# A two-layer encoder trunk on one core: the front end's weights in 20 buffers, 16 of them in the still empty gather ring, and 16 projections of the second block moved ahead of the first expert step

## The chip, the cores and the metric

The kernel runs on one core of a Trainium2 chip, in float32. The time is the device time of one execution in microseconds (us). Before the change it is 1650.69 us, the median of 3 runs (1648.89 to 1652.69).

The engines are TensorE (PE; PEld is its loading of weights), VectorE (DVE), ScalarE (ACT), GpSimd (POOL) and SyncE (SP). SP and ACT start plain transfers, POOL starts the indirect ones. All transfers run on the core's 16 DMA engines.

## The reference, cut to what matters

272 tokens (16 meta tokens and 256 of the input) of width 1024 pass through two layers. Each layer is a mixer and then a PEER layer, in which every token picks, for each of 8 heads, 16 of 16384 experts and reads their two rows of 1024 numbers.

```python
h = concatenate([meta, x])                         # 272 tokens, width 1024
for i in range(2):
    y = rmsnorm(h, mix_norm_g[i])
    h = h + (mixer_ab(y, ...) if i == 0 else mixer_conformer(y, ...))
    y = rmsnorm(h, ffn_norm_g[i])
    h = h + peer(y, peer_w_q[i], peer_sub_keys[i], peer_u[i], peer_v[i])
return rmsnorm(h, final_norm_g)[:, 16:272]

def mixer_ab(y, w_in, conv_w, w_out):
    q, k, v, gate_b, gate_c, h = split(y @ w_in, 6)  # w_in: 1024 x 3072
    a = stick_breaking_attention(q, k, v)            # 8 heads of 64
    b = gate_b * causal_conv3(gate_c * h, conv_w)
    return concat(a, b) @ w_out                      # 1024 x 1024

def peer(y, w_q, sub_keys, u, v):
    q = y @ w_q                                      # 1024 x 2048
    # top 16 of 128 keys on either side, top 16 of the 256 pairs -> expert, gate
    act = gate * gelu(sum(u[expert] * y))            # a dot of 1024 per expert
    return sum(act * v[expert])
```

## The kernel before, in words

**Layout.** Activations lie transposed: 128 partitions by (8 chunks of the width, tokens). A weight matrix of 1024 rows is cut into chunks of 128 columns, 512 KB each; one chunk is one transfer, and one projection of 8 matmuls (16 in the trace, where each float32 matmul has two records). The tokens are cut into a first block (A) of 128 and a second block (B) of 144.

**Front end.** The front end of block A runs alone: 24 chunks of the input projection (`inA`) with the attention between them, 8 of the output projection (`outA`), 16 of the query projection (`qA`). Then come the router's scores for the first 16 tokens (`scores(0)`, line 821 on PE), its top-k on DVE (`route_best`, `route_pairs`, `route_experts`, lines 1129 to 1185) and with `s_idx` the first gathers on POOL (line 382).

**Steps.** 33 steps `n` follow, 16 tokens each (16 tokens by 8 heads are the 128 partitions). A step takes 16 gathers of 1 MB into the ring `ring` of R = 12 slots. DVE makes a dot per gather (line 1191), ACT the gelu per quarter of a step (line 633), DVE the coefficients (lines 1202 and 1207), and PE sums the second halves of the rows (`values`, line 842), which frees 4 slots (`s_vm`). So gather `i` waits, from the 13th on, for the `values` of gather `i - 12`. `rows` (line 830) repeats the tokens of a step over the heads for the dots; `gates` (line 451) is the softmax's exponential on ACT, for which `route_pairs` of the next step waits.

**Work of block B beside the steps.** The table `FRONT` gives block B's front end quarter by quarter: `FRONT[u]` is issued by PE in quarter `u` (`u = 4 n + q`), and by ACT and DVE in the same order. Entries -3 to -1 run ahead of step 0. `inB` 0 to 11 stood there, `inB` 12 to 15 in quarters 0 and 1. Later the second layer's mixer runs in the same way (`side`).

**Weights.** `STREAM` lists all weight chunks in the order of use. SP walks it (line 352) with NB = 4 buffers (`wring`): a chunk's transfer waits until the projection that used its buffer is done (`s_proj`). The 16 chunks of `qA` alone had a place of their own, ring slots 4 to 11, and were started as 8 transfers of 1 MB between `inA` chunks (line 356). Slots 0 to 3 of the ring are block A's working memory until the gathers begin.

**Engine order.** Each engine has one fixed order of instructions; there is no scheduler. A wait holds everything that is behind it on its engine.

The lines that set this (the transfers' wait, then the gathers' wait):

```python
            for i, (row, job) in enumerate(STREAM):
                if i >= NB:
                    sp.wait_ge(s_proj, STREAM[i - NB][1] + 1)
                sp.dma_start(wring[:, i % NB, :, :]..., wall[row]).then_inc(s_w[i % NB], 16)
...
                    if i >= R:
                        pool.wait_ge(s_vm, i - R + 1)
```

## Time and profile before

| | |
|---|---|
| median of 3 runs | 1650.69 us |
| the profiled execution's own time | 1650.49 us |
| its span in the trace | 1648.7 us |
| busy: PE, DVE, ACT, POOL | 64%, 68%, 28%, 31% of the span |
| granted TensorE clock, mean of the span | 0.788 |
| moved by DMA | 649.84 MB, mean 394 GB/s |
| gathers | 528, 553.68 MB together |
| first gather issued | 126.50 us |

The time stands 1.8 us above the span, for what lies around it. The busy shares are means over stages with different limits, so they are read by stage: the front end up to 126.5 us, then the steps. "DMA" in a row is the mean busy share of the 16 DMA engines, and it can read slightly above 1.

### The profile page before, as it was taken

To read this page: it belongs to the slowest core of one execution; us is meant where nothing else is said; L and a number is where in the kernel's file an instruction comes from. 1 tells how busy PE (TensorE), PEld (TensorE's weight loads), DVE (VectorE), ACT (ScalarE), POOL (GpSimd) and SP (SyncE) were. 2 spreads that over 40 slices of the span, in tenths; PEclk is the share of its full clock that TensorE was granted. 3 is DMA by queue.
4 is the path that set the end of the run, shared out by engine and by line. 5 is a ranking of instruction groups with operands and counts; after the bars stand their busy time and mean duration, and the time that the engine had idled before them with its cause. 6 is when DMAs were issued, how large, how long until landed. Compare 5 with 4: busy or idle time off the path is not lost.

```text
span 1648.7 us, 19969 instructions
## 1 busy us (share of the span) xinstructions
PE 1048.9 (64%) x6936; PEld 710.0 (43%) x6936; DVE 1113.8 (68%) x3119; ACT 462.7 (28%) x953; POOL 503.8 (31%) x541
## 2 busy tenths in 40 slices
PE   7896777657744477776685456785766444544444
PEld 7896553434511156655463135664554111111111
DVE  2434658867557765887745766797756777777764
ACT  4101344302111133853221122873221211111110
POOL 0002323433233322332323332333323333333330
PEclk9999877878976689887897579887888655555666
DMA  9819999999999999899999999999999999999995
GB/s 333 328 65 394 418 420 386 421 419 419 417 420 422 421 419 414 348 411 384 417 417 417 422 420 417 371 401 398 411 418 418 422 421 422 421 422 421 419 421 212
DMA packets 105892, 649.84 MB, mean 394 GB/s; under 512 B 11456, under 2 KB 15552, under 8 KB 38208
## 3 DMA queue, kind: packets, MB, share of 16 engines
q0 software_dynamic: 76032, 553.68, 81.3%
q1 hardware_dynamic: 26272, 92.81, 14.5%
q10 hardware_dynamic: 3488, 2.08, 0.4%
q8 instruction: 55, 0.90, 0.2%
q14 instruction: 45, 0.37, 0.1%
HBM read 647.48 MB, written 1.05 MB: 393 GB/s over the span
## 4 chain that ended last, share of the span: by engine, by line
DMA 43%; PE 24%; DVE 16%; issue 5%; ACT 5%; POOL 5%; DVEq 2%; another core or an unknown queue 1%; POOLq 0%; ACTq 0%
DMA ring<-in_uv_dram,expert 31%; DMA wring<-in_wall_dram 12%; PE ps L659 10%; DVE ring L1191 7%; PE ps L842 7%; POOL ring L382 5%; ACT side L560 2%; PE ps L744 2%; DVE side L1246 2%; PE ps L855 1%; PE ps L666 1%; PE ps L883 1%; PE ps L830 1%; DVE picked L1183 1%
## 5 line engine op out<-in xcount | busy, mean ns | idle before, releaser
L1191 DVE CUSTOM_DVE_ANT_0 ring<-ring,ps 128x1024 f32<-128x1024 f32 x528 | 635.2, 1218 | 338.7 <-DMA ring<-in_uv_dram,expert 246.5
L382 POOL DMA_INDIRECT ring<-in_uv_dram,expert x528 | 501.8, 950 | 1110.9 <-PE ps L842 862.8
L842 PE MATMUL ps<-ring,mix 128*32 128x512 f32 x2112 | 366.3, 829 | 306.9 <-DVE mix L1207 303.8
L659 PE MATMUL ps<-yT,wring 128*128 128x128 f32 (+1 forms) x2048 | 279.0, 297 | 95.9 <-DMA wring<-in_wall_dram 58.5
L659 PEld LDWEIGHTS ps<-yT,wring 128*128 128x128 f32 x2048 | 262.9, 203 | 121.6 <-DMA wring<-in_wall_dram 64.8
L842 PEld LDWEIGHTS ps<-ring,mix 128*32 128x32 f32 x2112 | 67.8, 135 | 504.7 <-DVE mix L1207 364.4
L633 ACT ACTIVATE gel<-dots 128x4 f32<-128x4 f32 x132 | 27.1, 205 | 745.3 <-DVE dots L1191 667.6
L855 PE MATMUL ps<-sel,osb 128*128 128x16 f32 x528 | 76.9, 289 | 74.2 <-ACT osb L619 71.1
L855 PEld LDWEIGHTS ps<-sel,osb 128*128 128x128 f32 x528 | 73.6, 223 | 114.5 <-ACT osb L619 110.4
L560 ACT ACTIVATE side<-ident,params 128x128 f32<-128x128 f32 x310 | 97.3, 389 | 17.9 <-PE ps L883 16.3
L830 PE MATMUL ps<-ident,yg 128*128 128x128 f32 x264 | 52.3, 364 | 72.4 <-DVE dots L1191 72.4
L883 PE MATMUL ps<-side 128*128 128x128 f32 x620 | 85.5, 301 | 7.3 <-ACT side L560 6.7
L883 PEld LDWEIGHTS ps<-side 128*128 128x128 f32 x620 | 81.4, 214 | 16.3 <-issue 16.3
L830 PEld LDWEIGHTS ps<-ident,yg 128*128 128x128 f32 x264 | 44.0, 193 | 74.3 <-issue 74.1
L659 PE MATMUL ps<-side,wring 128*128 128x128 f32 (+1 forms) x512 | 67.8, 294 | 9.9 <-ACT side L586 7.9
L659 PEld LDWEIGHTS ps<-side,wring 128*128 128x128 f32 x512 | 65.1, 205 | 17.5 <-ACT side L586 9.7
L633 ACT ACT_TABLE_LOAD x51 | 65.4, 1283 | 1.5
L1246 DVE SCALAR_TENSOR_TENSOR side<-side,params 128x128 f32<-128x128 f32 x180 | 54.0, 347 | 0.0
L619 ACT COPY osb<-ps 128x1024 f32<-128x1024 f32 x33 | 33.3, 1009 | 46.2 <-PE ps L842 41.4
L1202 DVE SCALAR_TENSOR_TENSOR coef<-gel,grec,gexp 128x4 f32<-128x4 f32 x132 | 28.6, 217 | 24.3 <-ACT gel L633 20.3
L1191 DVE DVE_READ_ACCUMULATOR2_ANT dots<- 128x1 f32 x528 | 43.6, 83 | 0.0
L451 ACT ACT_TABLE_LOAD x33 | 42.3, 1283 | 0.9
(201 smaller groups left out, 954.4 us busy)
## 6 DMA issues: line engine op xcount, KB each, us to landing
wring<-in_wall_dram SPq DMA_DIRECT2D x160, 512.0 KB
ring<-in_uv_dram,expert POOLq DMA_INDIRECT x528
ring<-in_wall_dram SPq DMA_DIRECT2D x8, 1024.0 KB, 9.7
out_dram<-fo ACTq DMA_DIRECT2D x16, 64.0 KB
hT<-in_xT_dram ACTq DMA_DIRECT2D x1, 576.0 KB, 12.0
hT<-in_xT_dram SPq DMA_DIRECT2D x2, 256.0 KB, 5.0
params<-in_smalls_dram ACTq DMA_DIRECT2D x1, 430.0 KB, 4.4
```

What stands on the lines that cost most here:

```text
L382: pool.indirect_dma_start(out=ring[:, i % R, :], out_offset=None, in_=uv, in_offset=bass.IndirectOffsetOnAxis(ap=expert[:, n % 2, k:k + 1] ...
L451: act.activation(gexp[:, n % 2, :], topv[:, :], ACT.Exp, bias=negm[:, :], accum_out=gsum[:, n % 2:n % 2 + 1]).then_inc(s_exp, 1)
L560: act.activation(diag[:, j % NDIAG, :], ident[:, :], ACT.Identity, scale=convT[:, c, k:k + 1]).then_inc(s_dg, 1)
L619: act.copy(osb[:, :], po.rearrange("p a b -> p (a b)")).then_inc(s_oe, 1)
L633: act.activation(gel[:, 4 * q:4 * q + 4], dots[:, 4 * q:4 * q + 4], ACT.Gelu).then_inc(s_gel, 1)
L659: last = pe.matmul(ps[:, m % 2, 0:w], wring[:, i % NB, c, :], rhs(c), start=(c == 0), stop=(c == C - 1))
L830: last = pe.transpose(yrep[:, c * P:(c + 1) * P], yg[:, c, :, :].rearrange("p h t -> p (h t)"), ident[:, :])
L842: mm = pe.matmul(po[32 * j:32 * j + 32, half, :], mix[:, k, :], ring[:, slot, D + 512 * half:D + 512 * (half + 1)], start=(q == 0), stop=( ...
L855: last = pe.matmul(pt[:, c, :], osb[:, c * P:(c + 1) * P], sel4[:, :], start=True, stop=True)
L883: mm = pe.matmul(ps[:, m % 2, 0:P], diag[:, j % NDIAG, :], gz[:, c, o0 + k:o0 + k + P], start=(k == 0), stop=(k == CK - 1))
L1191: nc.vector.tensor_tensor_reduce(out=row, in0=row, in1=yrep, scale=1.0, scalar=0.0, op0=ALU.mult, op1=ALU.add, accum_out=dots[:, k:k + 1]) ...
L1246: ins = nc.vector.scalar_tensor_tensor(out=cv[:, c, :], in0=src, scalar=tap, in1=cv[:, c, :], op0=ALU.mult, op1=ALU.add)
```

## The change

The diff has four parts.

1. The weights of the front end go through 20 buffers: the 4 of `wring` and 16 in ring slots 4 to 11, two to a slot. `qA` joins `STREAM` (the 1 MB transfers and `s_wq` are gone). `BUFFER[i]` is the buffer of entry `i`: up to `EARLY` (the entry behind `inB` 15) they go round 20 buffers, so placed that `inB` 0 to 15 fall into the ring's 16; after it they go round the 4 of `wring`.
2. `FRONT` has quarters -4 to -1 with `inB` 0 to 15, four each; quarters 0 and 1 have no projections now. On ACT `gates(0)` comes behind all 16 instead of between them.
3. Gathers 4 to 11 wait for the second of the two `inB` projections whose weights lie in their slot (`FREE = 4`).
4. ACT starts only the first 100 columns of `params` at once; block B's part of `hT` (576 KB) and the other 760 columns (conv taps and keys) are started behind the two squares, and have `s_par2`.

```diff
-    FRONT = {-3: [("inB", k) for k in range(4)], -2: [("inB", k) for k in range(4, 8)], -1: [("inB", k) for k in range(8, 12)],
-             0: [("inB", 12), ("inB", 13)], 1: [("inB", 14), ("inB", 15)],
-             2: [("inB", 16), ("inB", 17), ("vt", 0), ("vt", 1)],
+    FRONT = {u: [("inB", 16 + 4 * u + k) for k in range(4)] for u in range(-4, 0)}
+    FRONT |= {2: [("inB", 16), ("inB", 17), ("vt", 0), ("vt", 1)],
@@
-    WQ0 = 32
+    STREAM += [(32 + k, JOB["qA", k]) for k in range(16)]
@@
+    FREE = 4
+    EARLY = LOADED[JOB["inB", 15]] + 1
+    BUFFER = [(i - EARLY) % (NB + 16) if i < EARLY else (i - EARLY) % NB for i in range(len(STREAM))]
+    BEFORE = [[j for j in range(i) if BUFFER[j] == BUFFER[i]] for i in range(len(STREAM))]
@@
+        def weights_at(i):
+            b = BUFFER[i]
+            if b < NB:
+                return wring[:, b, :, :]
+            return flat[:, (4 + b) * D:(5 + b) * D].rearrange("p (c n) -> p c n", n=P)
@@ sync
-                if i >= NB:
-                    sp.wait_ge(s_proj, STREAM[i - NB][1] + 1)
-                sp.dma_start(wring[:, i % NB, :, :].rearrange("p c n -> p (c n)"), wall[row]).then_inc(s_w[i % NB], 16)
-                if 8 <= i < 24 and i % 2 == 0:
-                    j = i // 2 - 4
-                    sp.dma_start(wq0[:, 2 * j:2 * j + 2, :, :].rearrange("p k c n -> p k (c n)"),
-                                 wall[WQ0 + 2 * j:WQ0 + 2 * j + 2].rearrange("k p n -> p k n")).then_inc(s_wq[j], 16)
+                if BEFORE[i]:
+                    sp.wait_ge(s_proj, STREAM[BEFORE[i][-1]][1] + 1)
+                sp.dma_start(weights_at(i).rearrange("p c n -> p (c n)"), wall[row]).then_inc(s_w[BUFFER[i]], 16)
@@ gpsimd
+                    elif i >= FREE:
+                        pool.wait_ge(s_proj, JOB["inB", 2 * (i - FREE) + 1] + 1)
@@ scalar
-            act.dma_start(params[:, :], smalls).then_inc(s_par, 16)
-            act.dma_start(hT[:, :, TA:L], ...).then_inc(s_x[2], 16)
+            act.dma_start(params[:, 0:PAR["conv"]], smalls[:, 0:PAR["conv"]]).then_inc(s_par, 16)
             for i in range(2): ...                     # the two squares
+            act.dma_start(hT[:, :, TA:L], ...).then_inc(s_x[2], 16)
+            act.dma_start(params[:, PAR["conv"]:NPAR], smalls[:, PAR["conv"]:NPAR]).then_inc(s_par2, 16)
@@
+            act.wait_ge(s_par2, 16)
             rows(0)
-            front(-3)
-            front(-2)
+            for u in range(-4, 0):
+                front(u)
             gates(0)
-            front(-1)
@@ tensor, ahead of the steps
+            pe.wait_ge(s_par2, 16)
             scores(0)
-            front(-3)
+            front(-4)
             scores(1)
             rows(0)
-            front(-2)
-            front(-1)
+            for u in range(-3, 0):
+                front(u)
```

PE before, from the last projections of `qA` (L744) to the second `values` (L842): L821 is `scores`, L830 `rows`, L659 with `yT` 128x144 the projections of block B, 8 matmuls each.

```order
L744 MATMUL ps<-ring 128x128 x120
L821 MATMUL ps<-params,qT 128x128 x2
L659 MATMUL ps<-yT,wring 128x144 x32
L821 MATMUL ps<-params,qT 128x128 x2
L830 MATMUL ps<-ident,yg 128x128 x8
L659 MATMUL ps<-yT,wring 128x144 x80
L842 MATMUL ps<-ring,mix 32x512 x8
L659 MATMUL ps<-yT,wring 128x144 x16
L842 MATMUL ps<-ring,mix 32x512 x8
L659 MATMUL ps<-yT,wring 128x144 x16
```

The same place of the changed kernel, whose line numbers are 3 to 9 higher (L668 is the projection, L845 `values`):

```order
L668 MATMUL ps<-ring,wring 128x128 x32
L824 MATMUL ps<-params,qT 128x128 x2
L668 MATMUL ps<-yT,ring 128x144 x32
L824 MATMUL ps<-params,qT 128x128 x2
L833 MATMUL ps<-ident,yg 128x128 x8
L668 MATMUL ps<-yT,ring 128x144 x96
L845 MATMUL ps<-ring,mix 32x512 x16
L668 MATMUL ps<-yT,wring 128x144 x16
```

Between `rows(0)` and the first `values` stand 12 projections instead of 10, and between the first two `values` none instead of 2.

POOL before, with the semaphores that each row waits for, from the last memset to step 1's first gathers:

```order
L374 MEMSET mix 128x512
L382 DMA ring<-in_uv_dram,expert 128x2048 [waits s_idx]
L382 DMA ring<-in_uv_dram,expert 128x2048 x11
L382 DMA ring<-in_uv_dram,expert 128x2048 [waits s_vm] x4
L382 DMA ring<-in_uv_dram,expert 128x2048 [waits s_vm,s_idx]
```

And in the changed kernel:

```order
L380 MEMSET mix 128x512
L391 DMA ring<-in_uv_dram,expert 128x2048 [waits s_idx]
L391 DMA ring<-in_uv_dram,expert 128x2048 x3
L391 DMA ring<-in_uv_dram,expert 128x2048 [waits s_proj] x8
L391 DMA ring<-in_uv_dram,expert 128x2048 [waits s_vm] x4
L391 DMA ring<-in_uv_dram,expert 128x2048 [waits s_vm,s_idx]
```

Eight of the first 12 gathers have got a wait on the projections.

ACT before, from the copy of `rows(0)` (L447) to the first gelu (L633), with L467 the emptying of an `inB` projection and L451 `gates(0)`:

```order
L447 COPY yg<-yT 128x1024 [waits s_y]
L467 COPY side<-ps 128x144 [waits s_proj] x8
L451 ACT_TABLE_LOAD
L451 ACTIVATE gexp,gsum<-topv,negm 128x16 [waits s_top]
L467 COPY side<-ps 128x144 [waits s_proj] x4
L447 COPY yg<-yT 128x1024 [waits s_yr,s_y]
L633 ACT_TABLE_LOAD
L633 ACTIVATE gel<-dots 128x4 [waits s_dot]
```

And in the changed kernel:

```order
L456 COPY yg<-yT 128x1024 [waits s_y,s_par2]
L476 COPY side<-ps 128x144 [waits s_proj] x16
L460 ACT_TABLE_LOAD
L460 ACTIVATE gexp,gsum<-topv,negm 128x16 [waits s_top]
L456 COPY yg<-yT 128x1024 [waits s_yr,s_y]
L642 ACT_TABLE_LOAD
L642 ACTIVATE gel<-dots 128x4 [waits s_dot] x3
```

`gates(0)` now follows 16 copies instead of 8, and nothing but the copy of `rows(1)` stands between it and the first gelu.

## Rows read from the trace of the kernel before

**Rows 1.** The page: GB/s in 40 slices of 41.2 us, and the gathers' queue.

```profile
GB/s 333 328 65 394 418 420 386 421 419 419 417 420 422 421 419 414 348 411 384 417 417 417 422 420 417 371 401 398 411 418 418 422 421 422 421 422 421 419 421 212
...
q0 software_dynamic: 76032, 553.68, 81.3%
```

**Rows 2.** Windows: busy us of PE, PEld, DVE, ACT, POOL, clock, DMA share, GB/s.

```profile
0.00:126.50 126.50, 112.23 (x942) 108.35 (x943) 45.31 (x151) 25.85 (x39) 1.77 (x12) 0.99 0.67 242
126.50:1648.70 1522.20, 936.70 (x5996) 601.68 (x5995) 1068.45 (x2969) 436.86 (x914) 502.07 (x529) 0.77 0.99 407
126.50:162.60 36.10, 23.68 (x164) 21.98 (x167) 14.88 (x47) 6.79 (x16) 11.44 (x12) 0.91 0.99 404
100.00:118.00 18.00, 17.52 (x156) 17.36 (x155) 3.68 (x16) 0.00 (x0) 0.00 (x0) 1.00 0.00 1
30.00:32.00 2.00, 2.00 (x13) 1.77 (x13) 0.29 (x1) 0.00 (x0) 0.00 (x0) 0.50 1.03 422
250.00:280.00 30.00, 19.04 (x116) 9.70 (x112) 27.57 (x76) 16.65 (x22) 11.81 (x12) 0.73 0.96 374
```

**Rows 3.** Waits up to 125 us; DVE in 193 to 248 (us, times, longest).

```profile
PEld ps L659 <- DMA wring<-in_wall_dram: 8.7, 7, 2.1
...
DVE ring L1191 <- DMA ring<-in_uv_dram,expert: 11.0, 8, 2.5
```

**Rows 4.** Timeline of PE: start, us, what, records, idle before.

```profile
9.69 10.88 PE L659 MATMUL ps<-yT,wring 128*128 128x128 f32 x96
...
28.69 2.67 PE L659 MATMUL ps<-yT,wring 128*128 128x128 f32 x16 [1.92 <-DMA wring<-in_wall_dram]
...
32.45 6.04 PE L659 MATMUL ps<-yT,wring 128*128 128x128 f32 x48
...
67.70 2.13 PE L719 MATMUL ps<-side,ones 128*128 128x144 f32 x16
...
116.16 0.68 PE L821 MATMUL ps<-params,qT 128*128 128x128 f32 x4 [0.47 <-DVE qT L1046]
...
161.78 1.92 PE L842 MATMUL ps<-ring,mix 128*32 128x512 f32 x16
...
259.90 3.64 PE L842 MATMUL ps<-ring,mix 128*32 128x512 f32 x16 [5.37 <-DVE mix L1207]
```

**Rows 5.** Timeline of DVE: start, then steps 0 to 2.

```profile
5.66 1.77 DVE L947 TENSOR_SCALAR yT<-hT,params 128x128 f32<-128x128 f32 x8 [5.66 <-DMA hT<-in_xT_dram]
...
126.04 0.17 DVE L1185 TENSOR_TENSOR expert<-picked 128x16 uint32<-128x16 f32 x1
...
148.89 0.14 DVE L1199 RECIPROCAL grec<-gsum 128x1 f32<-128x1 f32 x1
157.15 0.22 DVE L1202 SCALAR_TENSOR_TENSOR coef<-gel,grec,gexp 128x4 f32<-128x4 f32 x1 [8.11 <-ACT gel L633]
...
168.74 0.22 DVE L1202 SCALAR_TENSOR_TENSOR coef<-gel,grec,gexp 128x4 f32<-128x4 f32 x1
...
193.23 1.22 DVE L1191 CUSTOM_DVE_ANT_0 ring<-ring,ps 128x1024 f32<-128x1024 f32 x1 [1.46 <-PE ps L830]
...
247.83 1.22 DVE L1191 CUSTOM_DVE_ANT_0 ring<-ring,ps 128x1024 f32<-128x1024 f32 x1 [7.77 <-PE ps L830]
```

**Rows 6.** Timeline of POOL: gathers 0 and 12, and one of step 2.

```profile
126.50 1.09 POOL L382 DMA_INDIRECT ring<-in_uv_dram,expert  x1 [123.92 <-DVE expert L1185]
...
163.96 0.94 POOL L382 DMA_INDIRECT ring<-in_uv_dram,expert  x1 [22.66 <-PE ps L842]
...
263.80 0.94 POOL L382 DMA_INDIRECT ring<-in_uv_dram,expert  x1 [7.22 <-PE ps L842]
```

**Rows 7.** Timeline of ACT: an inB evacuation, and gates(0).

```profile
120.80 0.28 ACT L467 COPY side<-ps 128x144 f32<-128x144 f32 x1 [1.68 <-PE ps L659]
...
144.07 1.28 ACT L451 ACT_TABLE_LOAD   x1
```

**Rows 8.** The page's transfers: KB each, median us to landing.

```profile
hT<-in_xT_dram ACTq DMA_DIRECT2D x1, 576.0 KB, 12.0
```

More of the change, by code:

```diff
@@ L78, in hybrid_trunk @@
              9: [("av", 1), ("z", 6), ("z", 7), ("suf", 4), ("suf", 5)],
-             11: [("av", 2), ("suf", 6), ("suf", 7)], 13: [("av", 3)], 19: [("ssB", 0)]}
+              11: [("av", 2), ("suf", 6), ("suf", 7)], 13: [("av", 3)], 19: [("ssB", 0)]}
     for k in range(8):
@@ L113, in hybrid_trunk @@
                 STREAM.append((row + k, JOB[name % w, k]))
+    FREE = 4
+    EARLY = LOADED[JOB["inB", 15]] + 1
+    BUFFER = [(i - EARLY) % (NB + 16) if i < EARLY else (i - EARLY) % NB for i in range(len(STREAM))]
+    BEFORE = [[j for j in range(i) if BUFFER[j] == BUFFER[i]] for i in range(len(STREAM))]
+    assert all(BUFFER[LOADED[JOB["inB", k]]] == NB + k for k in range(16))
     ctx = ExitStack()
@@ L231, in hybrid_trunk @@
         ct = carve(AC, TA)
-        wq0 = flat[:, 8 * D:24 * D].rearrange("p (k c n) -> p k c n", c=C, n=P)
+        def weights_at(i):
[3 more added lines that the diff above has]
+            return flat[:, (4 + b) * D:(5 + b) * D].rearrange("p (c n) -> p c n", n=P)
         ps = ctx.enter_context(nc.psum_tensor("ps", [P, 8, 512], f32))
@@ L251, in hybrid_trunk @@
         s_par = sem("s_par")
-        s_w = [sem(f"s_w{b}") for b in range(NB)]
-        s_wq = [sem(f"s_wq{i}") for i in range(8)]
+        s_w = [sem(f"s_w{b}") for b in range(NB + 16)]
+        s_par2 = sem("s_par2")
         s_const = sem("s_const")
@@ L391, in _ @@
         def _(act):
-            act.dma_start(params[:, :], smalls).then_inc(s_par, 16)
-            act.dma_start(hT[:, :, TA:L], xT[:, C * TA:C * L].rearrange("p (c t) -> p c t", t=TB)).then_inc(s_x[2], 16)
+            act.dma_start(params[:, 0:PAR["conv"]], smalls[:, 0:PAR["conv"]]).then_inc(s_par, 16)
             for i in range(2):
@@ L400, in _ @@
                 act.activation(sq[:, cs, :], hT[:, cs, 0:TA], ACT.Square).then_inc(s_sq, 1)
+            act.dma_start(hT[:, :, TA:L], xT[:, C * TA:C * L].rearrange("p (c t) -> p c t", t=TB)).then_inc(s_x[2], 16)
+            act.dma_start(params[:, PAR["conv"]:NPAR], smalls[:, PAR["conv"]:NPAR]).then_inc(s_par2, 16)
             act.wait_ge(s_const, 6)
@@ L654, in chunk @@
                 i = LOADED[m]
-                pe.wait_ge(s_w[i % NB], 16 * (i // NB + 1))
+                pe.wait_ge(s_w[BUFFER[i]], 16 * (len(BEFORE[i]) + 1))
                 if m >= 2:
@@ L658, in chunk @@
                 for c in range(C):
-                    last = pe.matmul(ps[:, m % 2, 0:w], wring[:, i % NB, c, :], rhs(c), start=(c == 0), stop=(c == C - 1))
+                    last = pe.matmul(ps[:, m % 2, 0:w], weights_at(i)[:, c, :], rhs(c), start=(c == 0), stop=(c == C - 1))
                 last.then_inc(s_proj, 1)
@@ L736, in _ @@
             for k in range(16):
-                m = JOB["qA", k]
-                if k % 2 == 0:
-                    pe.wait_ge(s_wq[k // 2], 16)
                 if k == 0:
                     pe.wait_ge(s_hg2, C)
-                pe.wait_ge(s_bank[m % 2], m // 2)
-                for c in range(C):
-                    last = pe.matmul(ps[:, m % 2, 0:TA], wq0[:, k, c, :], hg2[:, c, :], start=(c == 0), stop=(c == C - 1))
-                last.then_inc(s_proj, 1)
+                chunk("qA", k, lambda c: hg2[:, c, :], TA)
                 if k == 0:
@@ L1021, in _ @@
                     log_weights(1)
+            dve.wait_ge(s_par2, 16)
             for c in range(C):
```

## The prediction, as it was put on record before the changed kernel ran

> **What bounds the kernel now.** I read the page first. Its row of GB/s [rows 1] shows 417 to 422 in most slices, with one hole, 65 in the third (82 to 124 us), and weaker slices later (386, 348, 371). I take 419 as the full rate. So I split the span where the first gather is issued, at 126.50 us [rows 6]: 242 GB/s before it and 407 behind it [rows 2]. Before it PE is busy 112.2 of 126.5 us, and from 100 to 118 us it is busy 17.5 of 18.0 us while DMA moves nothing. After it PE, DVE and ACT all have idle time and DMA has none to speak of (0.99). Two rules follow. In the front end TensorE sets the time. In the steps the bytes do: 528 gathers of 553.68/528 = 1.0486 MB [rows 1], 2.50 us each at the full rate, and each weight chunk of 0.524 MB, 1.25 us. A chunk that is moved out of the steps into the idle time before the first gather is worth 1.25 us, and a front end that ends earlier is worth what it ends earlier, as long as DMA doesn't run dry after it.
>
> **1. The front end, up to `scores(0)`, at 116.16 us before [rows 4].**
> - Start: PE begins behind the first half of `hT`, which DVE awaits until 5.66 us [rows 5]. It shares the engines with the 440 KB of `params`. Of these 51 KB are left, and 0.39 MB at the 350 to 400 GB/s of a loaded start is 1.0 us. Since they interleave I take 0.7 us off; bounds 0 and 1.3.
> - Weights: the loads of TensorE wait 8.7 us for `wring` in 7 waits, 2.1 the longest [rows 3]. They come about because four buffers are too few beside the eight 1 MB transfers that take half of the rate. With 20 buffers in the order of use, chunk k has landed at about 5 + 1.3 k us and is wanted at 9 + 1.8 k (96 records, 6 chunks, in 10.88 us [rows 4]). All 8.7 us go.
> - Clock: behind the wait of 1.92 us the granted clock is 0.50 in 30 to 32 us [rows 2]. That is 1.2 GHz, the lower level. There 16 records took 2.67 instead of 1.81 us and 48 took 6.04 instead of 5.44 [rows 4], 1.5 us together. Without the wait I take it off too.
> - What is late next: DVE. Between `inA` 13 and 19 four convolution chains and two weight steps lie on it, by the timeline nearly as long as PE's seven projections. I add 0.6 us; bounds 0 and 1.5. The stage has room for these terms: `inA` takes 67.70 - 9.69 = 58.0 us [rows 4], 24 chunks of 1.81 us are 43.4, and of the other 14.6 the waits and the clock are 10.2; the rest is the attention's own matmuls.
> - `outA` and `qA` run at PE's pace and keep it; taking `qA`'s weights from one buffer or another costs the same.
>
> Sum: -0.7 - 8.7 - 1.5 + 0.6 = -10.3 us (bounds -7 and -11.5). `scores(0)` stands at 105.9, the first index 10.0 us behind it as before (126.04 [rows 5]), the first gather at 116.2.
>
> **2. The 16 projections.** They take 1.96 us each (1.68 + 0.28 [rows 7]). Four run from 106.4 to 114.3, then `scores(1)` and `rows(0)`, 1.4 us, then twelve to 139.3. Before, PE made 10 of them by 161.8, waiting for weights that came between gathers.
> - Gather g (4 to 11) waits for `inB` 2(g-4)+1. Those end at 110.4, 114.3, 119.6, then every 3.9 us up to 139.3. The gathers are served every 2.50 us from about 118.3 (issue 1.1 us [rows 6], then about 1 us to the bytes, my estimate), so gather 11 has its turn only at 145.9. Each wait ends before its turn and costs nothing. Queued behind them on POOL are only later gathers.
> - `gates(0)` now stands behind all 16 on ACT, and DVE's `route_pairs(1)` waits for it. From its table load to DVE's reciprocal took 144.07 to 149.03 [rows 5, 7], 5.0 us. So 139.6 + 5.0 = 144.6, coefficients until 145.1 (12.4 us earlier than 157.15 [rows 5]), `values` at 145.2.
> - `values` to the gather that it frees took 2.2 us (161.78 to 163.96) with a fast clock and 3.9 us (259.90 to 263.80) behind 5.37 us of idle PE [rows 4, 6]. PE is idle for 5.9 us here, so 3.9: gather 12 is issued at 149.1, its bytes flow at 150.9, but the first twelve end at 148.4. **DMA is dry for about 2.5 us.** That is new.
> - Gathers 12 to 15 end at 160.9. Gather 16 needs the second `values`: 11.6 us behind the first on DVE (157.15 to 168.74 [rows 5], no gather awaited there), 156.9, + 3.9 = 160.8, bytes at 162.6. Dry again, 1.7 us. From there the weights of `inB` 20 on join and the freeing runs ahead. Bounds for both together: 0 and 9 us.
>
> **3. The bytes.** Before, 242 x 126.5 = 30.6 MB had moved at the first gather. The changed kernel has moved 68 chunks (48, 16, and `inB` 16 to 19 in `wring`) and 1.6 MB of inputs, 37.2 MB, at 116.2. I compare at 162.6: before 30.6 + 404 x 36.1 us = 45.2 MB [rows 2], changed 37.2 + 16 x 1.0486 = 54.0 MB. It is ahead by 8.8 MB, 21.0 us at 419 GB/s.
>
> **4. Does the lead survive?** Only if the chain over DVE, ACT and PE is as far ahead. Its first coefficients are 12.4 us earlier. Step 1's first dot came 24.5 us behind 168.74, with gather waits in it; kept whole it falls at 156.3 + 24.5 = 180.8, before at 193.23. Step 1 lasted 54.6 us to 247.83 [rows 5], of which DVE waited 11.0 us for gathers [rows 3]. Those have landed now, so step 2 starts at 224.4, 23.4 us earlier. The chain leads by more than DMA. Before, it was late there: 374 GB/s in 250 to 280 us [rows 2], (419 - 374) x 30 / 419 = 3.2 us lost. I take 2.5 us of them back (bounds 0 and 3.2). From step 3 on both kernels are the same, shifted; the weak slices later are made by chains that shift with it.
>
> Total: 1650.5 (the profiled execution's own time; the median is 0.2 us more) - 21.0 - 2.5 = **1627 us**. Ends: no dry time and all dips back, -5; front end at -7, no dips back, dry time doubled, +10. So 1621 to 1637.
>
> **The rivals.**
> - *The chain was the bound, not the bytes.* DMA's 0.99 then only shows queues kept full, and steps 0 and 1 keep their length: the gain is step 1's first dot, 12.4 us, 1638. For it: DVE waits 7.8 us for `rows` at 247.83 [rows 5] and DMA sags there. Against: DVE waited 11.0 us for gathers in the same step.
> - *The front end keeps its length.* The deep weight queue on SP starves block B's `hT`, which ACT now starts 5 us later, and ACT stands before the scores' copies: -10.3 shrinks to about -1, and as fewer gathers have been overtaken, 1636. For it: alone among the 4 first transfers it took 12.0 us to land [rows 8], and up to 16 chunks are ahead of it now. Against: in those 12 us it and `params` got 1.0 MB of some 4 (333 GB/s [rows 1]) beside a queue that was never empty; at that share it lands at about 15 us and is wanted at 20. The Trainium skill, "DMA: Bandwidth & Descriptors", section "Queues, rings and completion order", says that each DMA engine takes turns between the queues that have work, packet by packet, so a deep queue would not starve ACT's; the trace agrees as far as that share goes.
> - *Slower: the clock falls in the long dense run.* PE has 130 us without a gap, and if the clock is halved from `scores(0)` on, a projection takes 3.9 us. Each of the 16 that runs so delays the first `values` by 1.96 us, and DMA is dry for all of it, since only 12 gathers lie before it and the last of them wait too. All 16: 31 us, 1658. It is slower than before from the twelfth on. For it: 0.50 at 30 to 32 us, 0.73 in the steps [rows 2]. Against: the clock is 0.99 over the front end with PE 89% busy, and 1.00 in 100 to 118; each low value follows an idle PE. The Trainium skill, "TensorE: Matmul & The Clock Gate", section "Part 1: The HAM clock gate", puts it the same way round: the gate throttles an idle array and work opens it. By that page there is no such loss on one core, and by these rows neither.
> - *More than forecast:* no dry time and the later weak slices (348, 371) shrink as well: 12 us stand in these two, a third of them back and -5 give 1618.
>
> **How the numbers follow.** Forecast 0.60; the chain 0.12; the front end 0.10; more than forecast 0.11; the halved clock 0.04; something I have not thought of, near no change, 0.03. What the measurement can tell from no change is 0.2%, 3.3 us. Faster 0.93, same 0.02, slower 0.05. The range 1617 to 1638 takes in the forecast's 1621 to 1637, the front-end rival and half each of the chain's and of the larger gain.
>
> **What would show it.** In the profile of the changed kernel: no wait of PE for `wring` before 67 us and `scores(0)` at 104.7 to 109; the first gather 10.3 us behind it; DMA at full rate until about 148 us, then one or two gaps below 3 us each; the slice of 247 to 288 us at 410 or more; the same 407 to 410 GB/s behind the first gather, over a shorter stretch. I am wrong if waits for `s_proj` hold POOL while DMA is dry, if `gates(0)` delays the first `values` past 150 us, or if the span from the first gather to the end, 1522 us before, is not about 13 us shorter.

## The result

The changed kernel takes 1626.5 us (median of 4 runs, 1625.2 to 1627.5) where the kernel before takes 1649.8 (the 3 runs given above and one more, 1645.7 to 1652.7): ratio 0.986, 95% interval 0.984 to 0.988. The profiled execution took 1626.37 us, with a span of 1624.6. The forecast was 1627.

### The profile page after: what moved, and what is told of

Same layout as the page of the kernel before. It is cut to its first block, busy times and chain, and to the rows that moved or that the text cites. A ratio compares the mean times of both kernels' runs of the same rounds, so it can differ in the third digit from the quotient of the medians.

```text
span 1624.6 us, 19989 instructions
## 1 busy us (share of the span) xinstructions
PE 1046.7 (64%) x6936; PEld 712.2 (44%) x6936; DVE 1113.1 (69%) x3119; ACT 462.3 (28%) x953; POOL 502.6 (31%) x541
## 3 DMA queue, kind: packets, MB, share of 16 engines
q1 hardware_dynamic: 26400, 92.81, 14.7%
## 4 chain that ended last, share of the span: by engine, by line
DMA 40%; PE 26%; DVE 16%; POOL 5%; ACT 5%; issue 5%; DVEq 2%; POOLq 0%; ACTq 0%
DMA ring<-in_uv_dram,expert 33%; PE ps L668 13%; DMA wring<-in_wall_dram 8%; DVE ring L1197 7%; PE ps L845 7%; POOL ring L391 5%; ACT side L569 2%; PE ps L858 2%; DVE side L1252 2%; PE ps L675 1%; ACT L460 1%; PE ps L833 1%; DVE picked L1189 1%; DVE mix L1213 1%; PE ps L886 1%
## 5 line engine op out<-in xcount | busy, mean ns | idle before, releaser
L845 PE MATMUL ps<-ring,mix 128*32 128x512 f32 x2112 | 365.6, 827 | 311.4 <-DVE mix L1213 311.2
L845 PEld LDWEIGHTS ps<-ring,mix 128*32 128x32 f32 x2112 | 67.4, 134 | 509.7 <-DVE mix L1213 367.8
L668 PE MATMUL ps<-yT,wring 128*128 128x128 f32 (+1 forms) x1472 | 205.6, 301 | 71.8 <-DMA wring<-in_wall_dram 43.7
L668 PEld LDWEIGHTS ps<-yT,wring 128*128 128x128 f32 x1472 | 193.6, 207 | 94.6 <-DMA wring<-in_wall_dram 48.1
L858 PE MATMUL ps<-sel,osb 128*128 128x16 f32 x528 | 84.0, 304 | 78.6 <-ACT osb L628 78.6
L858 PEld LDWEIGHTS ps<-sel,osb 128*128 128x128 f32 x528 | 80.6, 241 | 116.7 <-ACT osb L628 116.7
L668 PE MATMUL ps<-yT,ring 128*128 128x128 f32 (+1 forms) x576 | 69.3, 282 | 0.0
L668 PEld LDWEIGHTS ps<-yT,ring 128*128 128x128 f32 x576 | 68.6, 193 | 1.2 <-issue 1.1
L668 PE MATMUL ps<-side,wring 128*128 128x128 f32 (+1 forms) x448 | 59.7, 296 | 10.7 <-ACT side L595 8.1
L668 PEld LDWEIGHTS ps<-side,wring 128*128 128x128 f32 x448 | 57.3, 206 | 17.9 <-ACT side L595 10.0
## 6 DMA issues: line engine op xcount, KB each, us to landing
ring<-in_wall_dram SPq DMA_DIRECT2D x52, 512.0 KB, 13.2
hT<-in_xT_dram ACTq DMA_DIRECT2D x1, 576.0 KB, 15.9
params<-in_smalls_dram ACTq DMA_DIRECT2D x1, 380.0 KB, 19.2
```

Of the source, the lines that this page charges most:

```text
L668: last = pe.matmul(ps[:, m % 2, 0:w], weights_at(i)[:, c, :], rhs(c), start=(c == 0), stop=(c == C - 1))
L845: mm = pe.matmul(po[32 * j:32 * j + 32, half, :], mix[:, k, :], ring[:, slot, D + 512 * half:D + 512 * (half + 1)], start=(q == 0), stop=( ...
L858: last = pe.matmul(pt[:, c, :], osb[:, c * P:(c + 1) * P], sel4[:, :], start=True, stop=True)
```

## The profile after

The page: GB/s in 40 slices (of 40.6 us), the gathers' queue, and two of the transfers of ACT's queue.

```profile
GB/s 371 355 230 380 417 411 408 419 421 417 418 422 421 421 418 417 352 421 407 420 416 421 421 419 417 353 409 394 415 418 405 422 422 422 421 422 422 421 421 194
...
q0 software_dynamic: 76032, 553.68, 82.4%
...
hT<-in_xT_dram ACTq DMA_DIRECT2D x1, 576.0 KB, 15.9
...
params<-in_smalls_dram ACTq DMA_DIRECT2D x1, 380.0 KB, 19.2
```

Against [rows 1] the third slice holds 230 GB/s instead of 65: that is the hole before the first gather, and most of what changed. The first two slices rose too (371 and 355 for 333 and 328), and the seventh (408 for 386); the fourth fell a little (380 for 394), and it holds the new dry time. The weak slices later (352 and 353 for 348 and 371) stand where they stood.

Windows (busy us of PE, PEld, DVE, ACT, POOL, clock, DMA share, GB/s):

```profile
0.00:116.00 116.00, 110.08 (x945) 107.88 (x946) 45.50 (x153) 25.73 (x39) 2.19 (x13) 1.00 0.87 322
116.00:1624.60 1508.60, 936.63 (x5993) 604.33 (x5991) 1067.63 (x2967) 436.54 (x914) 500.36 (x529) 0.76 0.99 406
116.00:162.60 46.60, 32.84 (x241) 26.68 (x240) 26.81 (x76) 7.65 (x19) 16.59 (x18) 0.82 0.92 364
30.00:32.00 2.00, 2.00 (x21) 2.00 (x20) 1.57 (x3) 1.97 (x3) 0.00 (x0) 1.00 1.03 412
140.00:170.00 30.00, 17.65 (x116) 9.86 (x117) 27.62 (x79) 5.37 (x14) 10.04 (x11) 0.72 0.93 365
230.00:270.00 40.00, 27.82 (x182) 15.82 (x182) 33.55 (x98) 20.27 (x29) 16.26 (x17) 0.83 0.99 401
```

322 GB/s over 116 us are 37.35 MB at the first gather, against 30.6 MB ten us later before [rows 2]. The clock of 30 to 32 us, 0.50 before, is 1.00. "Dry" below means that DMA has nothing to move, and "the dip" is the weak stretch of step 2. Two things are on the debit side: 365 GB/s in 140 to 170 us, which is (419 - 365) x 30 / 419 = 3.9 us of idle DMA that wasn't there before, and 401 in 230 to 270, 1.7 us, the rest of the dip that [rows 2] show with 374 in 250 to 280 (3.2 us).

Waits, first of PE and ACT up to 116 us, then of DVE from the first dot of step 1 to that of step 2 (us in total, times, longest):

```profile
ACT side L414 <- DMA hT<-in_xT_dram: 10.4, 1, 10.4
...
PE ps L668 <- DVE ring L1037: 0.6, 1, 0.6
...
DVE ring L1197 <- PE ps L833: 9.3, 2, 7.8
DVE ring L1197 <- DMA ring<-in_uv_dram,expert: 5.9, 4, 2.4
```

The wait for `wring` of [rows 3], 8.7 us, has no row left in the front end. What PE waits for in its place is DVE, 0.6 us.

Timeline of PE, rows that answer to [rows 4]:

```profile
8.32 7.85 PE L668 MATMUL ps<-yT,ring 128*128 128x128 f32 x64
...
20.32 3.84 PE L668 MATMUL ps<-yT,wring 128*128 128x128 f32 x32
...
56.79 1.39 PE L728 MATMUL ps<-side,ones 128*128 128x144 f32 x10
...
105.22 0.68 PE L824 MATMUL ps<-params,qT 128*128 128x128 f32 x4 [0.48 <-DVE qT L1052]
105.74 8.01 PE L668 MATMUL ps<-yT,ring 128*128 128x144 f32 x64
...
114.90 23.69 PE L668 MATMUL ps<-yT,ring 128*128 128x144 f32 x192
144.63 3.64 PE L845 MATMUL ps<-ring,mix 128*32 128x512 f32 x16 [6.04 <-DVE mix L1213]
155.99 3.64 PE L845 MATMUL ps<-ring,mix 128*32 128x512 f32 x16 [7.72 <-DVE mix L1213]
```

`inA` runs from 8.32 to 56.79, 48.5 us; before it took 58.0. From there to `scores(0)` they take 48.46 us before and 48.43 now. The twelve projections behind `rows(0)` run without a gap for 23.69 us. `values(0,0)` starts at 144.63, behind 6.04 us of idle PE.

Timeline of DVE (start; first index; reciprocal and two coefficients of step 0; first dots of steps 1 and 2), answering to [rows 5]:

```profile
4.08 1.66 DVE L951 TENSOR_SCALAR yT<-hT,params 128x128 f32<-128x128 f32 x8 [4.08 <-DMA hT<-in_xT_dram]
...
115.11 0.17 DVE L1191 TENSOR_TENSOR expert<-picked 128x16 uint32<-128x16 f32 x1
...
143.74 0.14 DVE L1205 RECIPROCAL grec<-gsum 128x1 f32<-128x1 f32 x1
143.96 0.22 DVE L1208 SCALAR_TENSOR_TENSOR coef<-gel,grec,gexp 128x4 f32<-128x4 f32 x1
...
155.42 0.21 DVE L1208 SCALAR_TENSOR_TENSOR coef<-gel,grec,gexp 128x4 f32<-128x4 f32 x1
...
173.87 1.22 DVE L1197 CUSTOM_DVE_ANT_0 ring<-ring,ps 128x1024 f32<-128x1024 f32 x1 [1.48 <-PE ps L833]
...
225.04 1.22 DVE L1197 CUSTOM_DVE_ANT_0 ring<-ring,ps 128x1024 f32<-128x1024 f32 x1 [7.77 <-PE ps L833]
```

Timeline of POOL, gathers 0, 11, 12 and 16 ([rows 6]):

```profile
115.57 1.09 POOL L391 DMA_INDIRECT ring<-in_uv_dram,expert  x1 [113.00 <-DVE expert L1191]
...
138.86 0.94 POOL L391 DMA_INDIRECT ring<-in_uv_dram,expert  x1 [2.98 <-PE ps L668]
148.49 0.94 POOL L391 DMA_INDIRECT ring<-in_uv_dram,expert  x1 [8.70 <-PE ps L845]
...
160.39 0.94 POOL L391 DMA_INDIRECT ring<-in_uv_dram,expert  x1 [7.24 <-PE ps L845]
```

Timeline of ACT: the square of block B's `hT`, and the table load of `gates(0)` ([rows 7, 8]):

```profile
20.70 1.16 ACT L414 ACTIVATE side<-hT 128x1152 f32<-128x1152 f32 x1 [10.42 <-DMA hT<-in_xT_dram]
...
138.92 1.28 ACT L460 ACT_TABLE_LOAD   x1
```

## The experiments

Three questions: is it the bytes or the chain (A), what is the order of the 16 projections worth (B), and what made the start earlier (C). e1 to e4, e5 to e8 and f1 to f4 ran on one chip each, beside the kernel before. The changed kernel's own ratio was 0.986 in the result, 0.9898 [0.9863, 0.9932] as e5_again, outside the 0.984 to 0.988 expected there, and 0.9871 [0.9850, 0.9892] as f1_after. The intervals overlap, so a difference between chips isn't certain, but kernels are compared within a chip. The changed kernel did not run on the chip of e1 to e4. Loss below means (419 - GB/s) x length / 419 of a window.

### A. Bytes or chain

**e1_front_end_only**: the 20 buffers and the order of loads stay, but only up to `qA`; `inB` is loaded and projected as before.

```diff
-    EARLY = LOADED[JOB["inB", 15]] + 1
+    EARLY = LOADED[JOB["qA", 15]] + 1
-                    elif i >= FREE:
-                        pool.wait_ge(s_proj, JOB["inB", 2 * (i - FREE) + 1] + 1)
```
`FRONT` and the order on ACT and PE are those of the kernel before (that part of the diff is left out).

> 20 buffers for the front end's 48 chunks alone; block B's 24 input chunks come through the 4 buffers again, with the old table and the old place of gates(0). Theory (the front end's length and the bytes behind the first gather are two separate gains): scores(0) at 105.2 us as in the changed kernel, but the bytes are back in the steps, so only the front end's 10.9 us are won: 1639 us (1637 to 1641). Rival (one gain, the early chunks; a shorter front end only makes the gathers wait for projections earlier): 1649. Rival (the chain was the bound in the steps, the bytes give nothing): within 2 us of the changed kernel, 1627.

Measured 1637.1 us against 1646.6 of before: ratio 0.9943 [0.9924, 0.9963], 9.5 us faster. `scores(0)` stood at 105.35. Less than the 10.9 by which the front end is shorter comes out, and two windows of e1 show where the rest went:

```profile
0.00:116.00 116.00, 110.18 (x944) 107.85 (x945) 45.46 (x153) 25.62 (x39) 2.06 (x13) 1.00 0.70 264
240.00:280.00 40.00, 29.77 (x178) 15.63 (x174) 33.12 (x96) 19.11 (x28) 15.58 (x16) 0.77 0.93 366
```

The dip now holds 366 GB/s, a loss of 5.1 us, 1.9 more than before. The front end's own part of the gain is about 9.5 us, and the rest of the change's has another source.

**e2_loads_early_old_front**: all loads as in the changed kernel; `FRONT` and the order on PE and ACT as before (`inB` 0 to 11 ahead of the first dots, `gates(0)` behind the eighth, 12 to 15 in quarters 0 and 1).

```diff
-    FRONT = {u: [("inB", 16 + 4 * u + k) for k in range(4)] for u in range(-4, 0)}
+    FRONT = {-3: [("inB", k) for k in range(4)], -2: [("inB", k) for k in range(4, 8)], -1: [("inB", k) for k in range(8, 12)],
+             0: [("inB", 12), ("inB", 13)], 1: [("inB", 14), ("inB", 15)]}
...
-            for u in range(-4, 0):
-                front(u)
+            front(-3)
+            front(-2)
             gates(0)
+            front(-1)
```

> The changed kernel's 20 buffers and early loads, but the projections in their old places: inB 0 to 11 ahead of step 0, 12 to 15 in its quarters 0 and 1, gates(0) between them. Theory (what counts is that the chunks are loaded early; making the last four projections ahead of the first dots only delays the first values): values(0, 0) near 136 instead of 144.6 us, gathers 11 and 12 issued by 142, DMA not dry at 148, so the 3.8 us lost between 140 and 170 us come back: 1623 us (1621 to 1625). Rival (the projections made ahead are a part of the gain): slower than the changed kernel, 1628 to 1632.

Measured 1621.6 us, ratio 0.9845 [0.9828, 0.9861]; 15.8 us less than e1 beside it (95%: 13.3 to 18.3). Up to 116 us e2 moves 322 GB/s where e1 moves 264: 6.7 MB, 16.1 us at the full rate. `values(0,0)` was forecast near 136 and started at 134.21, gathers 11 and 12 by 142 and were issued at 140.53 and 141.76. So loading `inB` early is worth its bytes, and making its projections earlier isn't needed for that.

One more thing differs between e1 and e2, and it would suit the chain rival: in e1 the projections wait for their weights, so its chain is late as well (`values(0,0)` at 146.35 us, 12.1 later than in e2). The run e3 below, on the same chip, parts the two. It has the early loads too, but its second coefficients on DVE, at 152.06 us, are only 5.0 us earlier than those of e1 (157.06), and yet it takes 14.7 us less (95%: 12.0 to 17.5). From these coefficients to step 1's first dot DVE waits in e1 for gathers (waits of DVE, 157 to 186.6 us),

```profile
DVE ring L1195 <- DMA ring<-in_uv_dram,expert: 9.9, 6, 2.3
```

and in e3 for none. So the chain of e1 is held up by the bytes, and the early chunks are what frees it.

**e5_again** is the changed kernel itself, run again as the base of the next three; **e6_bytes_back** loads as early as it does, and adds 32 half chunks (8.4 MB) of transfers to a scrap tile in the steps (164 to 479 us), which no computing engine reads. SP waits for each before it starts the next one.

```diff
                 sp.dma_start(weights_at(i).rearrange("p c n -> p (c n)"), wall[row]).then_inc(s_w[BUFFER[i]], 16)
+                if EARLY + 4 <= i < EARLY + 36:
+                    if i > EARLY + 4:
+                        sp.wait_ge(s_scrap, 16 * (i - EARLY - 4))
+                    sp.dma_start(scrap[:, :], wall[row][:, 0:D // 2]).then_inc(s_scrap, 16)
```

> The changed kernel once more, on the chip of the following three, so that they can be compared with it: 0.986 of before, as measured (0.984 to 0.988).

> The changed kernel with the bytes that it moved out of the steps put back as dead weight: behind each of 32 weight transfers of steps 0 to 7 SP starts a 256 KB copy (rows of 2 KB) into a place that nobody reads, 8.4 MB together. Nothing on PE, DVE, ACT or POOL changes. Theory (bytes behind the first gather set the time at 419 GB/s): 20.0 us more than the changed kernel. Rival (the chain over DVE, ACT and PE is the bound in these steps and DMA's queues are only kept full): 0 to 5 us more.

Measured 1635.3 (e5_again) and 1656.6 us (e6_bytes_back; 1.0023 [0.9999, 1.0046] of before, 1653.1): 21.3 us apart (18.1 to 24.5). 8.4 MB are 20.0 us. A chain that set the end would have swallowed most of it, if the run did nothing else to it. It did a little: SP's waits hold the next weight chunk too, and PE's waits for `wring` in 116 to 900 us rose from 19.1 to 28.9 us. So e6 alone doesn't part bytes and chain cleanly; with e3 against e1, where nothing was added, the chain rival falls.

### B. The order of the 16 projections

**e3_gates_first**: on ACT, `gates(0)` stands behind four of the 16 instead of behind all.

```diff
-            for u in range(-4, 0):
-                front(u)
+            front(-4)
             gates(0)
+            for u in range(-3, 0):
+                front(u)
```

> The changed kernel with gates(0) behind the first four projections' copies on ACT instead of behind all 16. Theory (the dry DMA of 140 to 170 us hangs on the first values, and these on gates(0)): values(0, 0) near 142 instead of 144.6 us, the first gap about gone, the second one a little longer, since gather 16 follows DVE: 1624.5 us (1623 to 1626). Rival (the short gaps are hidden elsewhere, later steps wait for other things): 1626.5, no change.

**e4_last_four_in_quarter_0**: as e3, and `inB` 12 to 15 are projected in quarter 0, behind `values(0,0)`.

```diff
-    FRONT = {u: [("inB", 16 + 4 * u + k) for k in range(4)] for u in range(-4, 0)}
+    FRONT = {u: [("inB", 16 + 4 * u + k) for k in range(4)] for u in range(-4, -1)}
+    FRONT[0] = [("inB", k) for k in range(12, 16)]
```
(`gates(0)` as in e3; the lines of ACT are left out.)

> gates(0) as in the run with it first, and inB 12 to 15 in quarter 0 of step 0: on PE they stand where they stood, ahead of values(0, 0), but ACT makes rows(1) and the first gelu before it empties them. Theory: values(0, 0) at about 138.7, right behind the last projection, with a fast clock; gather 12 at 141, gather 16 by 151; no gap: all 3.8 us come back, 1622.7 us (1621 to 1625). Rival (gaps are hidden elsewhere): 1626.5. Rival (PE waits for ACT to empty the banks behind the gelu, gathers 10 and 11 come late): 1628 or more.

Measured beside e2: e3 1622.4 us (0.9855 [0.9836, 0.9873]), e4 1620.0 (0.9842 [0.9824, 0.9861]). Timelines of PE (two rows of e3) and of PE and POOL (two of e4): `values(0,0)`, then `values(0,1)` of e3 and gather 12 of e4.

```profile
141.21 3.35 PE L846 MATMUL ps<-ring,mix 128*32 128x512 f32 x16 [3.48 <-DVE mix L1214]
152.64 3.64 PE L846 MATMUL ps<-ring,mix 128*32 128x512 f32 x16 [8.07 <-DVE mix L1214]
```

```profile
138.00 1.92 PE L847 MATMUL ps<-ring,mix 128*32 128x512 f32 x16
...
140.18 0.94 POOL L392 DMA_INDIRECT ring<-in_uv_dram,expert  x1 [0.90 <-PE ps L847]
```

In e3 the first `values` is 3.4 us earlier than in the changed kernel's profile, and gather 12 at 144.81 is in time; but PE is idle for 8.07 us before the second, since DVE had the same work before it, and gather 16 waits until 157.04: 386 GB/s in 140 to 170 us, a loss of 2.4 us. The stall moved from gather 12 to gather 16. In e4 the times came as forecast (138.00 for 138.7, gather 12 at 140.18 for 141, gather 16 at 150.45 for 151): gather 12 is issued 1.83 us behind gather 11, and the two windows show where its loss lies instead:

```profile
140.00:170.00 30.00, 20.75 (x144) 13.67 (x144) 23.76 (x66) 8.28 (x19) 13.30 (x14) 0.89 1.02 419
230.00:270.00 40.00, 28.73 (x176) 16.60 (x176) 32.72 (x93) 18.55 (x27) 14.89 (x16) 0.80 0.97 393
```

No idle DMA in 140 to 170, 2.5 us in 230 to 270 (in e3 the other way round, 420 there). The three orders are within each other's error on this chip (e3 - e2 +1.0 +- 2.4, e4 - e2 -1.3 +- 3.2 us), and the windows fit that: their losses in both places together are 3.7 (e2), 2.4 (e3) and 2.5 us (e4). Of the forecasts, e4's rival of 1628 or more falls; whether e3 and e4 gain on the changed kernel (1624.5 and 1622.7 against 1626.5) can't be told on this chip, where it did not run.

**e8_20_projections**: `inB` 16 to 19, which sit in `wring` at the first gather, are projected first, then 0 to 7, and 8 to 15 in quarters 0 and 1. So the four buffers come free and four more chunks are loaded before the gathers. `gates(0)` comes behind the first four; the entries of `inB` 16 to 19 in quarters 2 and 3 go (left out below).

```diff
+    FRONT = {-4: [("inB", k) for k in range(16, 20)], -3: [("inB", k) for k in range(4)], -2: [("inB", k) for k in range(4, 8)],
+             0: [("inB", k) for k in range(8, 14)], 1: [("inB", 14), ("inB", 15)]}
```

> One step further than the run with the last four in quarter 0: inB 16 to 19, whose weights wait in the 4 buffers, are projected first, right behind scores(0), so that inB 20 to 23 are loaded ahead of the first gather too; inB 0 to 7 follow, 8 to 13 stand in quarter 0 and 14 and 15 in quarter 1; gates(0) behind the first four. Theory (bytes and dry time): 4 chunks fewer behind the first gather are 5.0 us, but gather 11 waits for inB 15 until about 146 instead of 138 us, about 2 us of dry DMA: 3 us less than the run with the last four in quarter 0 (its ratio was 0.984). Rival (in step 2 the chain has become the bound, since DMA sags there to 339 GB/s): no gain or a loss, as the chain starts 4 us later.

Measured 1626.4 us, 0.9847 [0.9810, 0.9883], 9.3 +- 3.6 us less than e5_again beside it. It had 338 GB/s up to 116 us: 1.9 MB or 4.4 us more moved. By the same windows it loses 2.1 us less than e5_again in 116 to 140 us (397 against 360 GB/s), and 1.2 less in the two later ones (332 and 406 against 338 and 389): 7.7 us together. Part of that is that e5_again began 0.9 us late and was held up on the way (last section). Against the order of e4 the forecast of 3 us more failed: the ratio is 0.9847 where e4 had 0.9842, and 140 to 170 us lose 6.2 us (332 GB/s), not the 2 expected.

To compare the orders on one chip, the changed kernel and the kernels of e2, e4 and e8 were run again together:

> The changed kernel, unchanged, as the base for the three kernels beside it on one chip: the comparisons so far were made across chips. 22 to 24 us faster than before if its dry time behind gather 11 is about 4 us, as in its first profile; about 18 if it is 6 us, as on the second chip.

> All 64 early chunks and their buffers as in the changed kernel, but the projections in the old order (inB 0 to 11 ahead of the first dots, gates(0) behind the eighth). Theory (the bytes set the end, and the place of the 16 projections is worth only its dry time and its dips): it is as fast or up to 3 us faster than the changed kernel on the same chip, no dry time behind gather 11, a dip of 3 to 5 us' worth around 230 to 260 us. Rival (making the projections first is itself a gain, because the chain's work is out of the steps): 3 to 6 us slower than the changed kernel.

> Twelve of the 16 ahead of the first dots, the last four in quarter 0, gates(0) behind the first four. Theory: gather 12 is issued 8 us earlier than in the changed kernel, no dry time: 3 to 4.5 us faster than it on the same chip. Rival (the difference of the first call was one between chips): within 1.5 us of it.

> All 20 chunks that are loaded before the first gather are projected before or during quarters 0 and 1, so four more buffers come free early and four more weight chunks enter while gathers are not yet bound. Theory (bytes already on the chip count, not when they are used): within 1.5 us of the kernel with the last four in quarter 0. Rival (more work off the steps is more gain): 3 us or more faster than that one.

Before was 1653.9 us, so the changed kernel (f1) was 22.2 us faster by the medians, 21.8 +- 4.1 by the means; its six runs spread over 1626.2 to 1635.8 us. Loss (us) is worked out from one profile of each, the last column (us, 95%) from the means of the runs.

```
kernel                        median   ratio to before         loss 140-170  230-270  moved by 116 us  against f1
f1_after                      1631.7   0.9871 [0.9850,0.9892]      5.4        1.1      37.4 MB          -
f2_old_front_same_loads       1627.9   0.9843 [0.9826,0.9860]      0.1        2.4      37.4 MB       -3.5 +- 4.1
f3_last_four_in_quarter_0     1626.4   0.9828 [0.9810,0.9846]      0          3.3      37.4 MB       -6.0 +- 4.3
f4_20_projections             1628.0   0.9840 [0.9822,0.9858]      5.2        2.5      39.0 MB       -4.1 +- 4.3
```

The two windows of f1:

```profile
140.00:170.00 30.00, 16.22 (x96) 8.20 (x95) 25.92 (x73) 6.30 (x13) 8.66 (x10) 0.72 0.87 344
230.00:270.00 40.00, 27.76 (x172) 16.34 (x176) 32.76 (x94) 19.51 (x28) 15.09 (x16) 0.79 1.00 408
```

Of f3, with the idle time in the second instead of the first:

```profile
140.00:170.00 30.00, 23.86 (x160) 14.30 (x159) 24.45 (x69) 7.17 (x18) 12.39 (x13) 0.83 1.02 420
230.00:270.00 40.00, 29.08 (x176) 15.56 (x176) 33.57 (x99) 19.15 (x29) 15.22 (x17) 0.80 0.96 384
```

Of f4, up to the first gather and behind it:

```profile
0.00:116.00 116.00, 110.11 (x941) 107.79 (x942) 45.02 (x151) 27.01 (x41) 1.77 (x12) 1.00 0.92 336
140.00:170.00 30.00, 20.97 (x141) 13.39 (x139) 25.43 (x70) 4.36 (x15) 14.02 (x15) 0.84 0.88 347
```

The theory for f2 (0 to 3 us faster than the changed kernel) holds within its error, and the rival, that making the projections first is a gain in itself, falls: f2 isn't slower. f3 is faster than the changed kernel by more than the error. Its size of 6 us is above the 3 to 4.5 expected, by less than the interval. f4 has moved 1.6 MB (3.9 us) more by 116 us and gives it back in 140 to 170: gather 11 waits for `inB` 15, which now lies in quarter 1 (timeline of POOL in f4),

```profile
149.76 0.94 POOL L392 DMA_INDIRECT ring<-in_uv_dram,expert  x1 [5.03 <-PE ps L670]
```

and comes 9 us later than in f1 (140.65). It can't be told from f3 (+2.0 +- 3.1 us), and the rival, 3 us or more faster, falls. Bytes moved early count only if DMA isn't left dry to get them.

The best version found is that of e4 and f3: 0.9842 [0.9824, 0.9861] and 0.9828 [0.9810, 0.9846] of before on two chips, 26.6 and 27.5 us by the medians. Whether the orders of e2 (2.5 +- 2.6 us beside f3) and e8 are really behind it isn't settled.

### C. The start

**e7_inputs_at_start**: ACT issues the rest of `params` and block B's `hT` at once, as before.

```diff
             act.dma_start(params[:, 0:PAR["conv"]], smalls[:, 0:PAR["conv"]]).then_inc(s_par, 16)
+            act.dma_start(params[:, PAR["conv"]:NPAR], smalls[:, PAR["conv"]:NPAR]).then_inc(s_par2, 16)
+            act.dma_start(hT[:, :, TA:L], xT[:, C * TA:C * L].rearrange("p (c t) -> p c t", t=TB)).then_inc(s_x[2], 16)
```

> The changed kernel with the second half of params (389 KB) and block B's hT (576 KB) started at once again, ahead of the squares. Theory (the start gains what the 0.39 MB ahead of the first hT half cost): PE begins 0.7 to 1.5 us later (5.5 to 6.3 us instead of 4.8), scores(0) at 106 to 106.7, and the time is as much longer: 0.7 to 1.5 us more than the changed kernel. Against it stands that ACT waits 10.4 us for hT in the changed kernel: if that wait were on the path, this run would be faster.

Measured 1634.4 us, 1.8 +- 4.3 less than e5_again by the means: no difference that these runs could tell. In its profile PE starts at 4.81 us, with all of `params` and block B's `hT` started at once, and in e5_again, without them, at 5.67; `scores(0)` stands at 105.24 against 106.68. So the early start isn't bought by moving `params`; one and the same kernel begins at 4.78 (the result), 5.67 (e5_again) and 4.86 us (f1). What sets that is open, and since the kernel before (6.35 us) has one profile only, it isn't shown that the change made the start earlier.

## Why the prediction was right

**What bounds the kernel.** As read: TensorE the front end, bytes the steps. e6 (21.3 us for 8.4 MB) and e2 and e3 against e1 (15.8 and 14.7 us for 6.7 MB) show the second in both directions.

**Step 1, the front end.** Forecast -10.3, measured -10.94 (116.16 to 105.22). The start gave 1.4 instead of 0.7, outside my bounds of 0 to 1.3, and my reason for it (the 0.39 MB of `params` out of the way) fell in e7. The weights, the clock and DVE together: -9.6 forecast, 58.0 to 48.5 = -9.5 measured. The clock of 1.00 in 30 to 32 us, without the wait of PE, fits that the half clock came from that wait, and DVE as the next one late cost 0.6 us, as put.

**Step 2, the projections.** `values(0,0)` 145.2 forecast, 144.63 measured; gather 12 149.1 and 148.49; gather 16 160.8 and 160.39. Two dry stretches, 4.2 us together forecast, 3.9 measured in this profile, 5.4 (f1) and 5.8 (e5_again) in two later ones. Gather 11 was issued at 138.86 while DMA moved 418 to 431 GB/s from 125 to 145 us, so the waits of gathers 8 to 11, which are issued in that time, cost nothing; 4 to 7 were issued without a gap. In 116 to 140 us the changed kernel moved 374 GB/s where e2 moved 393, 1.1 us; nearly all of it lies in 120 to 125 us (336 against 419), and I can't place it. The dry time was rightly seen as the change's own cost, and e4 shows that it can be avoided.

**Step 3, the bytes.** Forecast 54.0 MB at 162.6 us; measured 37.35 + 364 x 46.6 us = 54.3 MB, ahead by 9.1 MB, 21.7 us (forecast 21.0).

**Step 4, the lead.** Step 2's first dot at 225.04, forecast 224.4; but that is luck, two errors that cancel. I kept the 24.5 us from the second coefficients to step 1's first dot, with the gather waits in them; they became 173.87 - 155.42 = 18.5, so the first dot came at 173.87 and not at 180.8. And I let all 11.0 us of gather waits go from step 1; 5.9 were left, and the step lasted 51.2 us, not 43.6. The two belong together: from the second coefficients to step 2's first dot DVE waited 16.8 us for gathers before (5.7, then 11.0 in step 1), and 5.9 now, all in step 1. That is 10.9 us less, and I had taken off 11.0; only their place was wrong. As I read it, the earlier the chain runs, the sooner it meets gathers again, so a wait for the bounding resource is shared out anew rather than gone; no run tests that by itself. So DVE's lead at step 2 was 22.8 us and DMA's 21.7, nearly the same, and the dip moved along. **This is the step that was mis-sized:** I took 2.5 of its 3.2 us back, and 1.5 came (3.2 to 1.7); the slice of 244 to 284 us shows 408 GB/s, where I had asked for 410 or more, and 406 behind the first gather where I had asked for 407 to 410. In e1, where only the front end is early, it even grew to 5.1.

**The sum.** By the profiled executions 24.1 us: 21.7 from the bytes at 162.6 us, 1.5 from the dip, and 0.9 in small differences I can't place. First gather to end is 1509.0 us, 13.2 less than before, forecast about 13. The lower end of the forecast's range was added up wrongly: 1627 less 5 is 1622, not 1621.

**The rivals.** The chain: fell (e3 against e1, and e6). The starved `hT`: its mechanism came, its price didn't. `hT` took 15.9 us and was there at 20.7, not at 15. ACT's square waited for it, and the copy behind the square (21.77 us, 20.47 in e7, where `hT` was there at 17.55) came 1.3 us late; PE had other work and didn't wait. The Trainium skill, "DMA: Bandwidth & Descriptors", section "Queues, rings and completion order", has each DMA engine take turns between queues packet by packet. I said that the trace agreed, and took the share that `hT` and `params` had had before, a quarter. It was smaller: in the 19.2 us until the larger part of `params` was there, ACT's queue got its 0.98 MB of some 7.5 (395 GB/s in 5 to 24 us), 13%. Turns by packet need not be equal shares of the bytes, and the queue rows of the profile's page (packets, MB) show unequal packets:

```profile
q1 hardware_dynamic: 26400, 92.81, 14.7%
q10 hardware_dynamic: 3632, 2.08, 0.4%
```

By its bytes q1 is SP's queue (176 chunks and the first `hT`) and q10 ACT's (`hT`, `params` and the output), so a packet has 3.5 KB on SP's and 0.57 KB on ACT's in the mean of the whole run. One packet of each in turn gives ACT 0.57 / (3.5 + 0.57) = 14%. That is an estimate that fits the 13%; no run here varies the packets, so it isn't shown to be the reason.

The halved clock: fell; the clock is 1.00 over the 116 us of the front end, and the 192 records of the twelve projections behind `rows(0)` took 23.69 us, 1.97 us for each projection. More than forecast: its half about the dry time came about in e4 (419 GB/s there), the one about the later slices nowhere.

## What to carry over

When a stage is bound by bytes and the one before it by compute, as here, the gain of an early load is about its bytes over the full rate, if DMA isn't left dry afterwards; look for buffers that are empty at that time, whatever their later owner. Then place the early work where it doesn't stand between the first results and what these free: here the last four projections, moved behind that point, and the gates, moved ahead of them, took away 4 to 5 us of idle DMA in 140 to 170 us, of which the later dip took back about 2 (1.1 to 3.3 us from f1 to f3). And when you take a wait for the bounding resource out of a chain, don't credit it all where it stood: count the waits from there to the next step together.
